# Fused two-block f32 transformer step on Trainium2: value and gate weights as 512-column products, gates drained ahead of the softmax, recurrence and residual scaling moved

## The reference, cut to what matters

```python
# block 1
h = rmsnorm(x, norm_g); proj = h @ w_in + b_in
u, v, za, ab, ab_gate, zb, g_a, g_b = split(proj)          # 8 x 1024 columns
y_a = gelu(u) * group_mix(layernorm(gelu(v))) * silu(za)
y_b = silu(groupnorm(conv31(ab * sigmoid(ab_gate)))) * silu(zb)
merged = sigmoid(g_a) * (y_a @ w_pa) + sigmoid(g_b) * (y_b @ w_pb)
x = x + merged @ w_out
x = x + sigmoid(rmsnorm(x) @ w_ple_gate) * (p @ w_ple); x = rmsnorm(x, final_g)
# block 2
xn = rmsnorm(x)
qa, ka, va, qb, kb, vb, qi, ki, wi, xc, yc, gates = split(xn @ w_in)   # va, vb 512 each, gates 3 x 1024
y_a = attention(qa, ka, va)                     # 8 heads of 64
y_b = top64_attention(qb, kb, vb, qi, ki, wi)   # 8 heads of 64, keys picked by an index score
y_c = rg_lru(conv4(xc)) * gelu(yc)              # a scan over the tokens, 512 channels
g = sigmoid(gates)
merged = g0 * (y_a @ w_pa) + g1 * (y_b @ w_pb) + g2 * (y_c @ w_pc)
x = x + merged @ w_o
x = x + square(relu(rmsnorm(x) @ w_up)) @ w_down; return rmsnorm(x, final_norm_g)
```

## Time and profile before

| | before |
|---|---|
| median of 3 runs | 772.01 us (771.97 to 772.43) |
| the profiled execution: time, span, granted clock | 772.69 us, 770.9 us, 0.997 |
| PE busy / weight loads | 97% / 92% of the span |
| DVE, ACT, POOL busy | 72%, 51%, 23% |
| DMA | 133.9 MB read, 179 GB/s mean |

### The profile page before, as it was taken

The page is one execution under the profiler, slowest core; times in us unless marked ns, Lnnn a source line. Parts: engine busy times, 40 slices in busy tenths (PEclk is TensorE's granted clock), DMA queues, the critical chain, the costliest instruction groups (busy, mean ns, idle before and its releaser), DMA issues. The chain is left out here.

```text
span 770.9 us, 13469 instructions
## 1 busy us (share of the span) xinstructions
PE 748.0 (97%) x5568; PEld 706.7 (92%) x5568; DVE 556.7 (72%) x879; ACT 393.7 (51%) x476; POOL 175.8 (23%) x109
## 2 busy tenths in 40 slices
PE   5999999999999998999999999999999999999996
PEld 5999999999999998999999899999999888888885
DVE  5396966999875786878898866566876755655564
ACT  6544545466562547653755455554347544354443
POOL 4898797971000010600013110000000000000000
PEclk9999999999999999999999999999999999999998
DMA  9866554546626587473554645535645465456521
GB/s 320 276 194 200 175 173 124 186 142 192 212 88 207 192 286 233 130 258 120 165 164 137 202 154 178 178 111 190 219 128 200 165 218 185 165 195 216 178 96 54
DMA packets 117384, 138.91 MB, mean 180 GB/s; under 512 B 4657, under 2 KB 107857, under 8 KB 117202
## 3 DMA queue, kind: packets, MB, share of 16 engines
q1 hardware_dynamic: 116706, 136.50, 54.9%
q0 software_dynamic: 480, 1.57, 0.8%
q10 hardware_dynamic: 144, 0.06, 0.0%
HBM read 133.93 MB, written 4.19 MB: 179 GB/s over the span
## 5 line engine op out<-in xcount | busy, mean ns | idle before, releaser
L507 ACT ACTIVATE s_whi<-s_raw 128x2048 fp32r<-128x2048 f32 (+1 forms) x93 | 174.2, 1875 | 52.0 <-PE sums L1460 28.4
L848 DVE TENSOR_TENSOR s_wlo<-s_raw,s_whi 128x2048 fp32r<-128x2048 f32 (+2 forms) x68 | 151.1, 2225 | 61.6 <-ACT s_whi L507 61.4
L1458 PE MATMUL sums<-s_a_parts,s_whi 128*128 128x256 f32 x576 | 163.5, 284 | 2.0 <-DVE s_wlo L848 2.0
L1459 PE MATMUL sums<-s_a_parts,s_whi 128*128 128x256 f32 x576 | 163.0, 283 | 0.0
L1460 PE MATMUL sums<-s_a_parts,s_wlo 128*128 128x256 f32 x576 | 163.0, 283 | 0.0
L1458 PE MATMUL sums<-s_b_hi,s_whi 128*128 128x256 f32 (+1 forms) x536 | 154.0, 287 | 0.8 <-DVE s_reg_d L1013 0.8
L1459 PE MATMUL sums<-s_b_lo,s_whi 128*128 128x256 f32 (+1 forms) x536 | 151.6, 283 | 0.0
L1460 PE MATMUL sums<-s_b_hi,s_wlo 128*128 128x256 f32 (+1 forms) x536 | 151.6, 283 | 0.0
L431 POOL TENSOR_TENSOR s_wlo<-s_raw,s_whi 128x1024 fp32r<-128x1024 f32 x52 | 128.2, 2494 | 28.0 <-ACT s_whi L507 27.8
L1458 PEld LDWEIGHTS sums<-s_a_parts,s_whi 128*128 128x128 f32 x576 | 110.6, 192 | 2.7 <-DVE s_wlo L848 2.2
L1459 PEld LDWEIGHTS sums<-s_a_parts,s_whi 128*128 128x128 f32 x576 | 110.6, 192 | 0.0
(11 more groups left out here) (310 smaller groups left out, 1297.7 us busy)
## 6 DMA issues: line engine op xcount, KB each, us to landing
s_raw<-in_w_in SPq DMA_DIRECT2D x61, 1024.0 KB, 5.7
s_raw<-in_w_up SPq DMA_DIRECT2D x16, 1024.0 KB, 5.5
s_raw<-in_w_down SPq DMA_DIRECT2D x16, 1024.0 KB, 6.8
s_raw<-in_w_pa SPq DMA_DIRECT2D x6, 1024.0 KB, 5.1
s_raw<-in_w_pb SPq DMA_DIRECT2D x6, 1024.0 KB, 5.5
s_raw<-in_w_out SPq DMA_DIRECT2D x4, 1024.0 KB, 5.2
s_raw<-in_w_ple_gate SPq DMA_DIRECT2D x4, 1024.0 KB, 7.4
s_raw<-in_w_o SPq DMA_DIRECT2D x4, 1024.0 KB, 5.7
```

What stands on the lines that cost most here:

```text
L507: act.activation(ring_view(whi, c), ring_view(raw, c), ACT.Copy).then_inc(Sm["hi_ready"], 1)
L848: ve.tensor_tensor(dst, src, part.bitcast(F32), ALU.subtract).then_inc(Sm["lo_ready"], 1)
L1458: pe.matmul(dst, sh, mh, start=first and k == 0, stop=False)
L1459: pe.matmul(dst, sh, ml, start=False, stop=False)
```

## The change

Weights of v, vb, va and g2 (`ROW_PAIRS`) are cut otherwise: a pair of units is 512 columns, the first unit its upper 512 rows, the second its lower 512 rows. Each unit multiplies both token halves with 512 columns moving, 24 matmuls instead of 48; half r of the pair goes to the bank of the pair's unit r, so unit 1's bank is needed halfway through unit 0 (`bank_free(c + 1)`). The drain of both banks comes once, after the second unit: v by ACT (gelu, 2 x 128x512), vb and va by DVE ahead of that iteration's `lo`, g2 by ACT, tanh straight from PSUM with a scale for each token (`rh_col`, half of `r_col`), ahead of the copies and exponentials. DVE's twelve multiplies of g2 go. The branches of the second block have 128 tokens stationary and 512 weight columns moving (24 matmuls a unit), `merged` stays with tokens as rows, and PE transposes it afterwards, 8 tiles in the middle of pa2's second unit and 8 behind the first four slices of wo's first unit; ACT and DVE split it from PSUM. The recurrence's first DVE multiplies go from c = 60 to 62, ACT's square root from 61 to 63, the scans and what follows from 62 and 63 to 65 to 69, `X3_AT` from 62 to 70. ACT's `hi` of units 88 and 89 now stands ahead of the split of `merged`, DVE's `lo` too.

```diff
-ACT_DRAINS = ("ab", "ag", "v", "u", "za", "zb", "ga", "gb", "up")
+ACT_DRAINS = ("ab", "ag", "v", "u", "za", "zb", "ga", "gb", "g2", "up")
+ROW_PAIRS = ("v", "vb", "va", "g2")
-X3_AT = 62
+X3_AT = 70
+SCAN_AT = 65
...
+            if kind in ROW_PAIRS:
+                w, col = (w1, off1["v"]) if kind == "v" else (w2, off2[kind])
+                col += 2 * S * (j // 2)
+                return w[:, KD // 2 * (j % 2):KD // 2 * (j % 2) + KD // 2, col:col + 2 * S]
...
 ACT
+                if now == "g2" and n % 2:
+                    act.wait_ge(Sm["multiplied"], c + 1)
...
+                    for r in range(NR):
+                        act.activation(gates2[:, r, S * (n - 1):S * (n + 1)], U[(c - 1 + r) % SLOTS][:, :], ACT.Tanh,
+                                       scale=rh_col[:, r:r + 1]).then_inc(Sm["act_drained"], 1)
...
-                if c == LRU_AT + 3:
+                if c == LRU_AT + 5:
...
-                if kind == "g2":
-                    act.wait_ge(Sm["dve_drained"], drained_count(c - 1))
...
 DVE
+                if kind in ("vb", "va") and j == 1:
+                    ve.wait_ge(Sm["multiplied"], d + 1)
+                    for r in range(NR):
+                        ve.tensor_scalar((vb if kind == "vb" else va)[:, r, :], U[(d - 1 + r) % SLOTS][:, :],
+                                         r_col[:, r:r + 1], None, ALU.mult).then_inc(Sm["dve_drained"], 1)
                 lo(c + 2)
...
-                elif kind == "g2":
...
-                    drain(d, two(tmp[:, j % 3, :]), bc)
...
+                if c == SCAN_AT:
+                    link(ve.tensor_tensor(lru_i, lru_i, lru_b, ALU.mult))
+                elif c in (SCAN_AT + 1, SCAN_AT + 2):
+                    for t in range(2 * (c - SCAN_AT - 1), 2 * (c - SCAN_AT)):
+                        ins = ve.tensor_tensor_scan(...)
+                elif c == SCAN_AT + 3:
+                    ve.tensor_tensor(lru_a, lru_r, yc, ALU.mult).then_inc(Sm["lru_dve"], 1)
+                elif c == SCAN_AT + 4:
+                    split_lo(c_lo[:, :, :], lru_a, c_hi[:, :, :], "yc_lo")
...
 PE
             def rows_out(c, h, l, bias=None):
+                half = UNITS[c][1] % 2
                 begin(c)
                 for r in range(NR):
-                    dst = U[c % SLOTS][:, S * r:S * r + S]
+                    if half == 0 and r == 1:
+                        bank_free(c + 1)
+                    dst = U[(c - half + r) % SLOTS][:, :]
...
-            def branch(c, h, l, t0):
+            def merged_rows_T(j):
+                pe.wait_ge(Sm["mg_added"], 4 + 2 * j + 2)
+                for n in (2 * j, 2 * j + 1):
+                    for k in (2 * n, 2 * n + 1):
+                        for r in range(NR):
+                            at = S * (k % 2) + P * r
+                            ins = rows_T(merged_rows, k, r, merged_T[n][:, at:at + P])
+                    ins.then_inc(Sm["m2_T"], 1)
+            def branch(c, h, l, t0, between=None):
...
-                for n in range(4):
...
+                for r, bank in enumerate((U[c % SLOTS], M[c % SLOTS])):
+                    ins = product(bank[:, :], row_tiles(h, l, r, t0), weights(c % SLOTS, 4, 0, 2 * S), 4)
+                    if r == 0:
+                        ins.then_inc(Sm["branch_half"], 1)
+                        if between is not None:
+                            between()
```

More of the change, by code:

```diff
@@ L750, in _ @@
             for j in range(6):
-                if j < 4:
-                    hi(FIRST["pc2"] + 3 + j)
+                hi(FIRST["pc2"] + 3 + j)
                 if j >= 4:
[L754 to L759, removed]
+                    for n in (2 * (j - 4), 2 * (j - 4) + 1):
+                        act.wait_ge(Sm["m2_T"], n + 1)
+                        act.activation(b_hi[:, 2 * n:2 * n + 2, :], merged_T[n][:, :].rearrange("p (t s) -> p t s", t=2),
+                                       ACT.Copy, scale=0.5).then_inc(Sm["m2_hi"], 1)
             for j in range(4):
@@ L1316, in _ @@
                 c = FIRST["pc2"] + n
[L1317 to L1318 removed]
+                g0 = D * {"pc2": 2, "pb2": 1, "pa2": 0}[kind]
+                cols = slice(2 * S * j, 2 * S * j + 2 * S)
                 for half in range(2):
[L1320 removed]
+                    if half == 0:
+                        ve.wait_ge(Sm["branch_half"], n + 1)
+                    else:
+                        ve.wait_ge(Sm["multiplied"], c + 1)
                     src = U[c % SLOTS] if half == 0 else M[c % SLOTS]
[L1322 to L1325 removed]
+                    by = gates2[:, half, g0 + 2 * S * j:g0 + 2 * S * j + 2 * S]
+                    dst = merged_rows[:, half, cols] if kind == "pc2" else tmp[:, half, :]
+                    ins = ve.scalar_tensor_tensor(dst, by, 1.0, src[:, :], ALU.add, ALU.mult)
                     if half == 0:
@@ L1332, in _ @@
                     for half in range(2):
-                        t = 4 * j + 2 * half
-                        tiles = merged[:, t:t + 2, :]
                         if half == 0:
@@ L1338, in _ @@
                             ve.wait_ge(Sm["dve_drained"], drained_count(c))
-                        ins = ve.tensor_tensor(tiles, tiles, two(tmp[:, half, :]), ALU.add)
+                        ins = ve.tensor_tensor(merged_rows[:, half, cols], merged_rows[:, half, cols], tmp[:, half, :],
+                                               ALU.add)
                         if kind == "pb2":
@@ L1343, in _ @@
                             ins.then_inc(Sm["mg_added"], 1)
-                    if kind == "pa2":
-                        for half in range(2):
-                            t = 4 * j + 2 * half
-                            ve.wait_ge(Sm["m2_hi"], 2 * j + half + 1)
-                            ve.scalar_tensor_tensor(b_lo[:, t:t + 2, :], merged[:, t:t + 2, :], 0.5,
-                                                    b_hi[:, t:t + 2, :].bitcast(F32), ALU.mult, ALU.subtract
-                                                    ).then_inc(Sm["m2_lo"], 1)
                 else:
@@ L1452, in begin, with product @@
                     pe.wait_ge(Sm[which], drained_count(b))
-            def product(dst, stationary, moving, kt, first=True):
+            def product(dst, stationary, moving, kt, first=True, last=True):
                 for k in range(kt):
@@ L1459, in product @@
                     pe.matmul(dst, sh, ml, start=False, stop=False)
-                    ins = pe.matmul(dst, sl, mh, start=False, stop=k == kt - 1)
+                    ins = pe.matmul(dst, sl, mh, start=False, stop=last and k == kt - 1)
                 return ins
@@ L1483, in columns, with arriving @@
                 ins.then_inc(Sm["multiplied"], 1)
-            def arriving(units, h, l, arrive, early=6, between=None, begin=begin):
+            def arriving(units, h, l, arrive, early=6, between=None, after=-1, begin=begin):
                 def tile_products(c, k):
@@ L1504, in arriving @@
                         tile_products(c, k)
-                if between is not None:
-                    between()
+                    if between is not None and c == units[after]:
+                        between()
                 for c in units:
```

115 lines of the change are left out of this document (53 added, 62 removed).

## The result

| | before | after |
|---|---|---|
| median (10 runs each) | 772.66 us (771.97 to 775.29) | 768.77 us (765.16 to 770.75) |
| ratio | 1 | 0.994, 95% interval 0.9927 to 0.9954 |
| profiled execution: time, span, clock | 772.69, 770.9, 0.997 | 769.60, 767.8, 0.998 |

What follows compares the result with a forecast made beforehand. PE, busy for 97% of the span, was taken to bound the kernel. −7.6 + 1.9 − 2.3 + 0.9 = −7.1 us from 772.69 gave 765.6, less 0.7 for the median: 764.9 us, range 763.4 to 768.0.

Steps and rivals of the forecast that it cites:

- Pace, −7.6: Units of v, vb, va, g2 and branches: matmuls of 512 columns at 0.2275 us replace pairs of 256, saving 7.6 us.
- Rival C: In the changed units 512 columns cost 0.23 to 0.24 us: 766.5 at 0.23, 772.5 if nothing is gained; chance 0.08.
- Transposes, +1.9: Sixteen f32 transposes of `merged` on PE, in two groups of eight, add 1.9 us (1.7 to 2.0).
- Stalls that go, −2.3: PE's waits on late DVE before the first scores (1.6 us) and for the first normalised probabilities (0.7) go.
- The stall that comes, +0.9: In unit 69, first of g2, the 13th matmul waits 0.9 us for DVE's first drain of va.
- Costed at nothing: Gelu timing, PE 1.1 us earlier at the convolution, g2's tanh, pa2's tail, the first recurrence and DMA: no cost.
- Rival D: v's 1.0 is given back before a DMA or DVE chain, or transposes wait 0.7: 765.6 to 766.5 us, chance 0.09.
- DMA bytes are the same: Under the items costed at nothing: the change leaves DMA bytes the same, with longer rows, so no time is added.

Runs made afterwards that it cites:

- after_sp2: The changed kernel with seven small loads moved behind unit 39's load, and the store wait with two bias loads behind unit 49's: 763.35 us, ratio 0.9873.
- before_sp2: The kernel before with the same seven loads, the store wait and two bias loads moved later in SyncE's order: 770.12 us, ratio 0.9959.
- sp1: Seven small loads in SyncE's queue moved behind unit 39's load: 764.06 us on the changed kernel, 773.63 on the kernel before.
- sp2: Seven small loads moved behind unit 39's load, store wait and two bias loads behind unit 49's: 763.35 us on the changed kernel, 770.12 on the kernel before.
- v_only: The kernel before with only the v part (v units as row pairs, gelu and statistics once a pair): 776.22 us, ratio 1.0035.
- no_v: The changed kernel with v as before (old drain and product): 766.27 us, ratio 0.9918.
- v_only_sp2: The v part alone on the kernel before, with seven small loads and the store wait moved later in SyncE's order: 768.83 us against 770.12 without the v part.
- before_pad56: The kernel before with 56 PE instructions that do nothing, in PE's idle time at the start: 777.23 us, ratio 1.0056.
- after_pad56: The changed kernel with 56 PE instructions that do nothing at the start: 768.62 us, against 768.77 for the changed kernel.

## Why the prediction was off

**Pace, −7.6: right.** A pair half of v after the change, 13 matmuls of 512 columns from one bias row to the next:

```profile
72.36 0.39 PE L1541 MATMUL sums<-s_b_hi,s_ones 128*128 128x512 f32 x1
...
75.33 0.39 PE L1541 MATMUL sums<-s_b_hi,s_ones 128*128 128x512 f32 x1
```

2.97 / 13 = 0.228, the 0.2275 of the earlier trace rows. Rival C and the rule of the Trainium skill's page "TensorE: Matmul & The Clock Gate" (section "Back-to-back issue gap"), which it gives for the isolated matmul and by which 1.6 us would be saved instead of 7.6, are out. From the start of v to its end the gain was 1.1; in the profiled execution PE came to v 0.3 us later than before, hence the 0.8 at 107 us. In after_sp2, where PE is 1.1 earlier behind v, 0.3 of it goes to a wait for ACT at a group norm (0.33 at 214.6).

**Transposes, +1.9: right.** Timeline of PE after, the first group:

```profile
553.33 1.04 PE L1449 MATMUL misc<-s_ident,s_reg_f 128*128 128x128 f32 x8
554.12 0.48 PE L1471 MATMUL misc<-s_whi,s_a_parts 128*128 128x512 f32 x1
```

0.79 a group and 0.1 for the slow first matmul behind it, 1.8 for both. No wait ahead of either.

**Stalls that go, −2.3: right**, both are out of the list. In the pair before_sp2 and after_sp2, which nothing else disturbs, the difference grows from −0.8 at the group norm to −3.8 at the first transposed probabilities: 0.6 of it is the pace of vb, 2.4 the stalls.

**The stall that comes, +0.9: right**, with the cause named. PE and DVE after, in unit 69:

```profile
442.76 0.39 PE L1473 MATMUL sums<-s_whi,s_b_lo 128*128 128x512 f32 x1
443.84 0.50 PE L1471 MATMUL sums<-s_whi,s_b_hi 128*128 128x512 f32 x1 [0.69 <-DVE s_reg_w L1214]
```

```profile
441.91 1.21 DVE L1312 TENSOR_TENSOR s_abc<-s_abc,s_reg_s 128x1024 f32<-128x1024 f32 x1
443.05 1.40 DVE L1214 TENSOR_SCALAR s_reg_w<-sums,s_r_col 128x512 f32<-128x512 f32 x2
```

From the 12th to the 13th matmul it is 1.08 instead of 0.23, and 0.1 more for the next one; taken away, 1.3 us came back in the median and 1.0 in the traces.

**The step that failed** stands under "Costed at nothing": that PE "may be 1.1 us earlier without waiting", since the convolution's result is 4.0 us early. That slack is real, and no wait came there. But I stopped at that wait. From 229 us on this part of the first block hangs on SyncE's queue: the load of unit 38 behind seven small ones, then the store that blocks unit 47. I also passed over the 2.0 us wait of the earlier trace rows as lying "in a part that the change doesn't touch"; it was the sign that PE has no reserve there. In the profiled executions the `s_wlo` waits between 240 and 310 us sum to 5.2 us after and 2.5 before: 2.7 lost. Besides the idle time, the steps from matmul to matmul around such a wait are 0.10 to 0.16 longer than in a steady stream, which sums to 0.9 more than before. Together that is the 3.6 us by which PE went from 0.8 earlier to 2.9 later. Rival D named the place (v's gain "given back in front of a chain that hangs on DMA") with 1 us; the price was 4 (2.9 lost instead of 1.1 gained), since I held the transfers' lengths for fixed. "DMA bytes are the same" was true and not enough.

Shown: the loss lies in the transfers (sp1, sp2), the v part brings it (v_only, no_v, v_only_sp2), and moving PE's program alone can bring it too (before_pad56). Not settled: whether the fetch is the whole cause of the late load. after_pad56 kept a load of 7.2 with the fetch out of the way, so the arrival 0.7 us earlier (R3) may have a part. The v part also changes the shape of v's own loads (longer rows, half as many); these land long before 229 us, and no run tests whether they matter.

The medians differ by 3.9 and not by the traces' 3.1, since single executions vary. Of the 3.9 us between the forecast 764.9 and the measured 768.77, 3.2 are the change (3.9 for 7.1), and 0.7 the reference: the three runs of before that the forecast started from lie at its low end (772.01; the median of ten is 772.66).

## What to carry to other kernels

Look for the place where PE's few waits lie, however small their sum: there a gain from upstream ends. In a queue of DMA issues, what waits for a late result must not stand ahead of loads whose buffer is free; moving seven small loads was worth nothing in the kernel before and 4.7 us in the changed one, more than the change itself had brought. When instructions go, compare transfer lengths in both traces, not only bytes: the same load took 5.8 and 8.5 us. And a wait of PE can cost more than its length, through the clock behind it.

## What the runs showed of the hardware

56 PE instructions that do nothing, in time that was idle, made the kernel 4.6 us slower (777.23 against 772.59): the packets of the instruction queue moved by 5 us (240.2 to 235.0), a 64 KB load grew from 2.4 to 4.3 us and the 3 MB store from 10.2 to 11.9. A second execution of it on another chip showed the same lengths (4.3 and 12.0) but was only 1.7 us slower than the kernel before beside it (774.45 against 772.79), since the clock stayed up. And after an idle time of 2.4 us the granted clock of TensorE fell to 0.5 for 3.4 us in some executions of a program and not in others.
